# Two blocks of a transformer on one core: a first chunk on x times weight at two norms, squares before held splits, a later transpose, and a shifted activation tensor

## The reference

```python
for i in range(2):                                   # first block
    h = rmsnorm(x, norm_mix[i])
    x = x + (even_mixer(h, ...) if i % 2 == 0 else odd_mixer(h, ...))
    x = x + conv_ffn(rmsnorm(x, norm_ffn[i]), w_up, conv_w, conv_b, w_down)
for l in range(2):                                   # second block
    h = rms_norm(x, ln1_g[l]) * (1 + sc1) + sh1
    x = x + g1 * (merged(h) @ w_out[l])
    h2 = rms_norm(x, ln2_g[l]) * (1 + sc2) + sh2
    x = x + g2 * (square(relu(h2 @ w_ff1[l])) @ w_ff2[l])
return rms_norm(x, final_g)

def rmsnorm(x, g):
    return x * rsqrt(mean(x * x, axis=-1) + EPS) * g
```

## Time and profile before

| | |
|---|---|
| Median of 3 runs | 1359.36 us (1359.27 to 1366.26) |
| The profiled execution | 1361.97 us |
| Its span | 1360.2 us |
| Mean granted clock of TensorE | 0.996 |
| PE busy | 1321.4 us (97%), 10934 matmuls |
| DVE busy | 979.9 us (72%) |
| ACT busy | 739.4 us (54%) |
| POOL busy | 319.0 us (23%) |
| Chain that ended last | PE 81%, DVE 12%, ACT 4% |

### The profile page before, as it was taken

How to read it: one execution, slowest core, us unless ns; L and a number is a source line. 1 busy time by engine, 2 the same in 40 slices (tenths; PEclk the granted TensorE clock), 3 DMA queues, 4 the chain that set the end, 5 groups by cost and what they waited for, 6 DMA issues and landing times.

```text
span 1360.2 us, 25618 instructions
## 1 busy us (share of the span) xinstructions
PE 1321.4 (97%) x10934; PEld 1280.8 (94%) x10934; DVE 979.9 (72%) x1214; ACT 739.4 (54%) x952; POOL 319.0 (23%) x165
## 2 busy tenths in 40 slices
PE   7999999999999999999999999999999999999997
PEld 6888999999999999999999999999999999999997
DVE  6965799975577489996658776999765877644442
ACT  6646666555565465555455656544345564655432
POOL 5000055500000015530015001773001500177200
PEclk9999999999999999999999999999999999999999
DMA  8333667775645457766344446889934544555550
GB/s 301 125 124 124 264 251 260 264 278 187 217 168 183 146 187 276 279 253 245 125 176 165 155 164 226 292 309 341 364 133 152 183 162 138 177 202 197 186 186 31
DMA packets 40865, 278.72 MB, mean 205 GB/s; under 512 B 4656, under 2 KB 5168, under 8 KB 9264
## 3 DMA queue, kind: packets, MB, share of 16 engines
q1 hardware_dynamic: 33696, 226.23, 46.8%
q10 hardware_dynamic: 7056, 50.86, 10.2%
HBM read 276.02 MB, written 1.05 MB: 204 GB/s over the span
## 4 chain that ended last, share of the span: by engine, by line
PE 81%; DVE 12%; ACT 4%; issue 2%; DMA 0%; SPq 0%; DVEq 0%; ACTq 0%
PE bank L844 22%; PE bank L845 22%; PE bank L846 22%; DVE low L1548 5%; DVE adax L1901 2%; PE bank L810 2%; PE bank L803 2%; PE bank L804 2%; ACT high L1154 1%; PE bank L822 1%; PE bank L823 1%; PE bank L824 1%; PE bank L887 1%; PE bank L1119 1%; PE bank L1090 1%
## 5 line engine op out<-in xcount | busy, mean ns | idle before, releaser
L1548 DVE TENSOR_TENSOR low<-raw,high 128x2048 fp32r<-128x2048 f32 (+3 forms) x223 | 497.0, 2231 | 209.6 <-ACT high L1154 206.2
L844 PE MATMUL bank<-op_high,low 128*128 128x256 f32 (+2 forms) x1928 | 543.9, 282 | 4.8 <-DVE low L1548 4.0
L845 PE MATMUL bank<-op_low,high 128*128 128x256 f32 (+2 forms) x1928 | 535.8, 278 | 0.0
L846 PE MATMUL bank<-op_high,high 128*128 128x256 f32 (+2 forms) x1928 | 535.7, 278 | 0.0
L1154 ACT ACTIVATE high<-raw 128x2048 fp32r<-128x2048 f32 (+3 forms) x223 | 407.0, 1826 | 142.3 <-PE bank L846 131.5
L844 PEld LDWEIGHTS bank<-op_high,low 128*128 128x128 f32 (+2 forms) x1928 | 362.1, 188 | 11.2 <-DVE low L1548 6.8
L845 PEld LDWEIGHTS bank<-op_low,high 128*128 128x128 f32 (+2 forms) x1928 | 360.9, 187 | 3.1 <-issue 2.4
L846 PEld LDWEIGHTS bank<-op_high,high 128*128 128x128 f32 (+2 forms) x1928 | 360.6, 187 | 0.3
L844 PE MATMUL bank<-act_high,low 128*128 128x256 f32 x864 | 241.8, 280 | 0.7 <-DVE low L1548 0.7
L846 PE MATMUL bank<-act_high,high 128*128 128x256 f32 x864 | 241.1, 279 | 0.0
L845 PE MATMUL bank<-act_low,high 128*128 128x256 f32 x864 | 241.1, 279 | 0.0
(11 more groups left out here) (304 smaller groups left out, 1801.3 us busy)
## 6 DMA issues: line engine op xcount, KB each, us to landing
raw<-stream SPq DMA_DIRECT2D x197, 1024.0 KB, 5.0
adaw<-ada ACTq DMA_DIRECT2D x28, 1024.0 KB, 6.4
adax<-ada ACTq DMA_DIRECT2D x20, 1024.0 KB, 6.2
raw<-stream SPq DMA_DIRECT2D x10, 768.0 KB, 5.9
raw<-stream SPq DMA_DIRECT2D x10, 512.0 KB, 3.5
raw<-stream SPq DMA_DIRECT2D x2, 640.0 KB, 4.0
x<-xT SPq DMA_DIRECT2D x2, 512.0 KB, 4.5
out<-h SPq DMA_DIRECT2D x1, 1024.0 KB, 3.9
```

The source lines that it names most:

```text
L844: pe.matmul(o, wl[:, w], oh[:, k, :], start=one, stop=False, skip_group_check=True)
L845: pe.matmul(o, wh[:, w], ol[:, k, :], start=False, stop=False, skip_group_check=True)
L846: mm = pe.matmul(o, wh[:, w], oh[:, k, :], start=False, stop=end, skip_group_check=True)
L1548: dve.tensor_tensor(low[m % SPLIT][:, at:w], raw[m % RAW][:, at:w], high[m % SPLIT][:, at:w], ALU.subtract).then_inc(S["low_ready"], 1)
```

## The change

Five things change.

- **First chunk on x times weight (norms 1 and 2).** Chunks up0g0 and od000 no longer wait for the norm. Their operand is the split of x times the norm's weight, without the factor rstd that each token has: ACT rounds it (`high_of_gain`), DVE subtracts (`gain_low`), pair by pair, in the projection before. It lies in blocks 13 to 20 of AH and AL, and in two new tensors, third_high and third_low. Their products are multiplied by rstd afterwards, by one DVE operation of 128 x 512 from PSUM into `first_out`, blocks 0 and 1 of h; everything that read these two chunks' bank reads first_out. The last two `sumsq` products stand in the middle of this chunk. up0v0 and od001 become the first chunks that take the normed operand, without the 10 BUSY products.
- **Splits around these norms.** ACT's `high` of the chunk three further on moves ahead of the last two roundings of the norm, and DVE's `low` of it goes from the end of the norm to the head of the next chunk's stage, ahead of the new multiplication. The sums and the norm of unit 8 (the heads of od000) come after the products of od010, together with those of unit 9, instead of after those of od001; its sums go to bank TB. Two PSUM rings are turned.
- **Squares ahead of held splits.** Behind odo1 and odo2 the `high` of the chunk three further on comes after the squares and x times weight of that pair, not before.
- **ket later.** The transposes of the keys go from ahead of chunk av0 to behind it.
- **Squared activations at 0 modulo 512.** The 32 words of `line2` are gone, so act2_high and act2_low start at 132,608 and 165,376, both multiples of 512, and relu and adax are 128 bytes lower.

```diff
 RINGS = {
...
-    "od0": (0, 1, 2, SB0, SB1),
-    "od1": (1, 2, OB, 0),
+    "od0": (2, 0, 1, SB0, SB1),
+    "od1": (1, OB, 0, 2),
...
-        f("line2", [P, 32])
         BH = f("act2_high", [P, 32, TOK], F32R)
...
+        FIRST = {"up0g0": 1, "od000": 2}
+        GAIN_HIGH = (None, AH[:, 13:21, :], GH2)
+        GAIN_LOW = (None, AL[:, 13:21, :], GL2)
+        first_out = h[:, 0:2, :]
+        BEHIND_NORM = ("bq0", "up0v0", "od001", "up1g0", "cq0a", "fa0_0", "cq1a", "fa1_0")
...
                 c(name, split=not held)
-                if held:
-                    st_("high", name)
                 if pair > behind:
...
                 if BY[name]["last"]:
                     st_("square", (i, pair)), st_("square_add", (i, pair))
-                    if pair < 3:
+                    if pair < 3 or i in (1, 2):
                         st_("xg", (i, pair))
                     pair += 1
+                if held:
+                    st_("high", name)
...
-            st_("sumsq", (i, 3))
+            if i >= 3:
+                st_("sumsq", (i, 3))
...
-        c("ak", split=False), each("diff_p", 2, 3), st_("diff_n", 0), st_("high", "ak"), sw("diff", 4, 5), st_("ket")
+        c("ak", split=False), each("diff_p", 2, 3), st_("diff_n", 0), st_("high", "ak"), sw("diff", 4, 5)
         st_("low", "ak")
-        c("av0", split=False), st_("unit", 4), each("diff_t", 4, 5), st_("high", "av0"), sw("diff", 6, 7), st_("low", "av0")
+        c("av0", split=False), st_("ket"), st_("unit", 4), each("diff_t", 4, 5), st_("high", "av0"), sw("diff", 6, 7), st_("low", "av0")
...
                     for at in range(0, len(turns), 2):
                         some = turns[at:at + 2]
+                        if name in FIRST and at == len(turns) // 2:
+                            sumsq((FIRST[name], 3))
...
+            def high_of_gain(i, k):
+                g, _ = gain_and_shift(i)
+                return act.activation(GAIN_HIGH[i][:, k, :], x[:, k, :], ACT.Copy, scale=g[:, k:k + 1])
...
+                elif i < 3:
+                    dve.wait_ge(S["gain_high"], 4 * (i - 1) + p + 1)
+                    g, _ = gain_and_shift(i)
+                    for k in (2 * p, 2 * p + 1):
+                        ins = dve.scalar_tensor_tensor(out=GAIN_LOW[i][:, k, :], in0=x[:, k, :], scalar=g[:, k:k + 1],
+                                                       in1=GAIN_HIGH[i][:, k, :], op0=ALU.mult, op1=ALU.subtract)
+                    ins.then_inc(S["gain_low"], 1)
...
+                if name in FIRST:
+                    low_upto(n + SPLIT - 1)
+                    dve.wait_ge(S["products_done"], n + 1)
+                    dve.tensor_tensor(first_out, ps[b][:], rn[:].rearrange("p (a b) -> p a b", a=1)
+                                      .to_broadcast([P, 2, TOK]), ALU.mult).then_inc(S["first_scaled"], 1)
```

More of the change, by code:

```diff
@@ L292, in build @@
         adaw = [sb(f"adaw{i}", [P, 2, D], F32, adaln) for i in range(3)]
+        third = ExitStack()
+        sb("below_third", [P, 11264], F32, third)
+        GH2 = sb("third_high", [P, KB, TOK], F32R, third)
+        GL2 = sb("third_low", [P, KB, TOK], F32R, third)
+        third.close()
         ffn = ExitStack()
@@ L380, in build @@
         MLA_OUT = (OB, NB)
-        BEHIND_NORM = ("bq0", "up0g0", "od000", "up1g0", "cq0a", "fa0_0", "cq1a", "fa1_0")
+        FIRST = {"up0g0": 1, "od000": 2}
[3 more added lines that the diff above has]
+        BEHIND_NORM = ("bq0", "up0v0", "od001", "up1g0", "cq0a", "fa0_0", "cq1a", "fa1_0")
         def gain_and_shift(i):
@@ L522, in odd_step @@
                 st_("dil_t", (turn, 0))
+            if unit == 9:
+                st_("unit", 8)
             if unit is not None:
@@ L723, in operand_wait @@
                     return S["operand_low"], lambda k: FILLS["mix0"] + MIX_ORDER.index(k) // 2 + 1
-                if name in ("up0g0", "up1g0"):
+                if name in ("up0v0", "up1g0"):
                     return S["operand_low"], lambda k: FILLS["n1" if name[2] == "0" else "n3"] + k // 2 + 1
-                if name == "od000":
+                if name == "od001":
                     return S["operand_low"], lambda k: FILLS["n2"] + k // 2 + 1
@@ L784, in high_part_first @@
                     blocks = range(ncols // P)
-                    if name in BEHIND_NORM:
+                    if name in BEHIND_NORM and name not in ("up0v0", "od001"):
                         for _ in range(BUSY):
@@ L1156, in high_upto, with squares_of @@
                     split_to[0] += 1
-            def squares_of(u, bank):
+            def squares_of(u, src):
                 if u >= 2:
                     act.wait_ge(S["unit_sums"], u - 1)
-                act.activation(sq[u % 2][:], ps[bank][:], ACT.Square).then_inc(S["unit_squares"], 1)
+                act.activation(sq[u % 2][:], src, ACT.Square).then_inc(S["unit_squares"], 1)
             def unit(u):
@@ L1175, in chunk @@
                     return
-                if not (name.startswith("pa") and name.endswith("1")):
+                b = bank_of(ch)
+                src = first_out if name in FIRST else ps[b]
+                if name in FIRST:
+                    act.wait_ge(S["first_scaled"], FIRST[name])
+                elif not (name.startswith("pa") and name.endswith("1")):
                     act.wait_ge(S["products_done"], n + 1)
-                b = bank_of(ch)
                 if name in ("av0", "av1"):
```

56 lines of the change are left out of this document (38 added, 18 removed).

## The result

The changed kernel took **1354.48 us** (median of 11 runs, 1351.38 to 1358.71), the kernel before 1361.58 us (11 runs, 1358.47 to 1367.84). The ratio is **0.9945, 95% interval 0.9928 to 0.9961**: 0.55% faster, which is 7.5 us by the ratio and 7.1 by the medians. The forecast was 1349.3 us, with a gain of 10.1. The profiled execution took 1352.04 us, span 1350.2; its like before took 1361.97.

What follows compares the result with a forecast made beforehand. PE, busy 97% of the span, was taken as the bound, through its pace of issue. The terms -7.1 - 1.8 - 1.9 + 1.2 - 0.5 = -10.1 us, from the median 1359.36, gave 1349.3 us; range 1342 to 1358.

Steps and rivals of the forecast that it cites:

- The bound for "faster": Whole kernel: a time below 1352.6 us counts as faster, about 0.5% or 6.8 us from no change; chance 0.55.
- Part 1: fb0 and fb1: squared activations at 0 modulo 512 make 1536 matmuls 4.6 ns quicker each, gain 7.1 us, bounds 0 and 7.1.
- the turn at 1259.40: Where fa1 ends and fb1 begins: pace goes from 113.0 to 116.9 ns a matmul, with only the moving operand changed.
- the chance that fb0 and fb1 are in it: Rival in fb0 and fb1: the shift fails, pace depends on how the stream began; 1356.4 us, or 1352.8 if one stage; chance 0.2.
- The page: Skill page with SBUF lines of 16 bytes: read as saying the shift changes nothing, making the sum 7.1 us smaller.
- Parts 2 and 3: Norms 1 and 2: first chunks up0g0 and od000 run before the norm is ready, gains 1.8 and 1.9 us.
- the waits forecast at norm 1: PE waits 0.4 us for up0v0's pair 2, 0.8 for up0g1's split and 0.3 ahead of up0v1.
- 3.9 if none of the three waits comes: Norm 1: upper bound of the gain, 3.9 us, against 1.8 taken; lower bound 0.
- The first-layer rival: up0 and down0 fall to the slow pace, 7.3 us more, 1356.6 us alone; chance 0.25.
- Part 4: Norm 3: with squares ahead of splits, the square of block 6 comes later and the norm too, loss 1.2 us.
- Part 5: ket: PE's 1.16 us wait for scaled keys partly goes, gain 0.5 us, bounds 0 and 1.2.
- The second layer's stream: Rival: up1 and down1 become quick after norm 3, 7.3 us more gain, 1342.0 us; chance 0.2.

Runs made afterwards that it cites:

- 3: The change with line2 put back, so all parts but the shift: 1358.85 us, ratio 0.9981 to the kernel before.
- 4: The kernel before with only the squares put ahead of the held splits of odo1 and odo2: 1362.29 us, ratio 1.0027.
- 6: The kernel before with only ket turned one chunk later, behind av0's products: 1359.54 us, ratio 1.0009.
- 8: The change with four extra products of 32 weight columns ahead of ten chunks: 1351.44 us, ratio 0.9935 to the kernel before.
- 12: The change with one extra 32-column product ahead of ten chunks and the squares behind the held splits again: 1349.18 us, ratio 0.9908 to the kernel before.
- 1: The kernel before with only line2 taken out, the shift alone: 1358.48 us, ratio 0.9979.
- 2: The kernel before with line1 at 48 words, operands 128 bytes further (op and act at 128 modulo 512, act2 at 256): 1368.9 us, ratio 1.0064.
- 11: The change with op_high and all behind it moved on by 256 bytes, weights still at 64: 1357.12 us, ratio 0.9958 to the kernel before.
- 7: The change with the weights high, low and raw moved from 64 to 0 modulo 512 bytes: 1396.47 us, ratio 1.0263 to the kernel before.
- 5: The kernel before with only the first chunk on x times weight behind norms 1 and 2: 1357.42 us, ratio 0.9969.
- 9: The change with the weights high, low and raw at 448 modulo 512 bytes: 1371.37 us, ratio 1.0069 to the kernel before.

## Why the prediction was right, and where it was off

- **Whole.** 1354.48 lies in the range of 1342 to 1358. It is 5.2 us above the forecast: 2.2 because 1349.3 stood on a median of three runs that was that much below the later one, and 3.0 because the gain by the medians was 7.1 and not 10.1. The bound for "faster" was put at 1352.6, which the time misses; against its own runs of the kernel before it is 0.55% faster, just over the 0.5% that the bound stood for. That the two profiled executions lie 9.9 us apart, almost the 10.1 of the sum, is luck: fb1 and fa1 came out slow and up1 and down1 quick.
- **Part 1, the shift: right in kind, wrong in size.** The sentence that failed is "I take 7.1, since the turn at 1259.40 had no other cause". The shift did cause that turn: it takes the pair of operands from distance 64, where the stream was slow in all 160 chunks of fb, to 192, where it can be quick. With a quick fa1, fb1 starts slow at 64 (before, 3, 4, 6) and quick at 192 (8, 12). But I had read the slow aligned stages as an upset that lasts, and still put the chance that fb0 and fb1 are in it at 0.2. In the profiled runs at distance 192 fb was quick in 0 of 32 chunks (1), 19 of 32 (the change), 26 (8), 29 (12) and, at 256, 29 (2) and 16 (11). By the times the shift is worth 3 to 5 us, of which the 3, from 1, is not clear of noise.
- **The page.** The Trainium skill, SBUF — State Buffer, Door 1: The DMA port swizzle, gives lines of 16 bytes; that a shift by 128 bytes then changes nothing was my inference. It fails for TensorE's reads: with op and act 128 bytes further all 100 chunks of up, down and fa were slow (2), and 64 bytes on the weights cost 42 us (7).
- **Parts 2 and 3.** -1.46 and -2.15 against -1.8 and -1.9; in 5 they were worth -1.66 and -2.15. Of the waits forecast at norm 1 (0.4, 0.8, 0.3) came 0.23, 0.69, 0.18, so 0.4 us less in all. What was left out took it back: the first sum waited 0.37 us longer for DVE's `square_add`, behind the operations that were added there (0.15 longer in 5), which the forecast had at nothing, and up0g1 ran at the slow pace for one chunk (0.21 us), after which the stream was quick. The bound "3.9 if none of the three waits comes" was added up wrong: 1.8 and the three waits are 3.3. The first-layer rival (0.25) did not come in any profiled run at distance 192 but 11, where up0 and down0 were slow in 29 of 34 chunks.
- **Part 4.** +1.24 in 4, as forecast, by the mechanism forecast; +0.77 in the change. The square of block 6 waits 1.8 us longer and the first sum 0.7 less, both as added up. This part of the change should be left out.
- **Part 5.** 0.5 forecast; 0.16 measured to ag0's end, and in 6 nothing (+0.09) to av1's end. What I had named as late next, the copy of the turned keys, was late by 1.1 us, nearly all of the wait. I took half of a gap where the row of the next link should have been added up.
- **The second layer's stream**, a rival at 0.2, is what happened in the profiled run: up1 was quick in the change and in 3, 4, 5 and 6, slow before and in 1 and 11. Neither 4 nor 6 has the early chunks, and 6 touches no norm at all, so parts 2 to 4 are not what picks it. That it is drawn anew in each execution fits the spread of the runs of one kernel (18 us in 1), which was 3 us in 8 and 5.8 in 12. But 7, all of whose chunks had one pace in the profile, still spread over 5.5 us and 9 over 9.7, so part of the spread has another cause; and I have one profile of each kernel, so the draw itself isn't shown.

## What to carry to other kernels

Where PE is busy 97% of the time, count the starts in equal windows of each stage before anything else: up1 and down1 going from 172 to 179 in 20 us was worth 5.9 us here, more than the 3.0 of the four other parts together. Look at the start of both operands, the one that moves and the one that is held, and try several distances between them; here leaving out 64 bytes of padding ahead of the weights took the ratio from 0.9945 to 1.0263. A gain seen in one pair of profiled executions may be a draw: price it by the stretches that the edit touches, and by many runs.

## What the runs showed of the hardware that I had not expected

- Products of 128 x 128 by 256 in fp32r start 113.3, 117.8, 118.4 to 120.2 or 120.0 ns apart at full clock, by the distance modulo 256 bytes between the partition offsets of weights and moving operand, and at distances 192 and 64 by a state as well. That it is a collision of the two reads would fit, but is only argued: no counter shows it.
- A single product with 32 weight columns ended the slow state in three of three cases, for 0.11 us, and four in a row in two of two.
- The granted clock falls to half, 1.2 GHz, for stretches of 3.4 us, behind idle time on PE. A stretch in 12 (22 products in 4 us; the clock column is 0.57):

```profile
80.00:84.00 4.00, 4.00 (x22) 4.00 (x22) 3.55 (x13) 3.16 (x9) 0.00 (x0) 0.57 0.54 227
```

  Each costs at most about 1.7 us, an estimate: half of its 3.4 us, where PE is busy throughout. Ahead of the last 10 us the kernel before had two, the change one, 4 and 5 three, 12 four, 8 and 9 none. Which idle gap brings one varies: behind the wait for ket, the same 1.2 us in length, 4 and 5 had one (the two chunks behind it took 1.5 us longer) and the kernel before had none. With ket later that wait is gone, but its own gap can bring one as well (12, at 80 us).
